# First pointwise weights kept in DRAM as two parts, three GpSimd convolution tiles and a layer norm spread over the last products

## The reference, cut to what matters

```python
mixed = concatenate([gla_o, hgrn_o, xo]) * silu(gate)       # 2048 wide
x = x + mixed @ w_out                                       # end of the first block; x = rms_norm(x)
mod = silu(c) @ w_mod + b_mod                               # six vectors of 1024
h = modulate(rms_norm_2(x, norm1_g), sh1, s1)
u = h @ w_pw1 + b_pw1                                       # 1024 -> 2048
a, gate = split(u); u = a * sigmoid(gate)
u = dwconv(u, w_dw) + b_dw                                  # 31 taps, in segments of 64 tokens
u = silu(layer_norm(u, ln_g, ln_b))
x = x + g1 * (u @ w_pw2 + b_pw2)
x = x + g2 * (square(relu(modulate(rms_norm_2(x), sh2, s2) @ w1)) @ w2)
```

## Time and profile before

| | before |
|---|---|
| median of 3 runs | 2215.16 us |
| profiled execution | 2215.97 us, its span 2214.2 us |
| PE busy | 2074.0 us (94%), 10286 matmuls |
| DVE busy | 1173.6 us (53%) |
| POOL busy | 867.5 us (39%) |
| ACT busy | 675.7 us (31%) |
| DMA | 171.59 MB, 77 GB/s over the span |

### The profile page before, as it was taken

One profiled execution on the slowest core, in us unless ns is written; L12 is line 12 of the kernel. 1 busy time (PEld: TensorE's weight loads), 2 busy tenths in 40 slices (PEclk: granted clock), 3 DMA queues, 4 the chain that ended last, 5 costly groups with the idle time before them and its releaser, 6 DMA issues.

```text
span 2214.2 us, 26275 instructions
## 1 busy us (share of the span) xinstructions
PE 2074.0 (94%) x10286; PEld 1728.3 (78%) x10286; DVE 1173.6 (53%) x1977; ACT 675.7 (31%) x1200; POOL 867.5 (39%) x511
## 2 busy tenths in 40 slices
PE   7899999898998889999989987899899999999997
PEld 5779988787887768888867866678778888888886
DVE  5353455456463346775578877989634222222226
ACT  2312322211036510010345436464433322212212
POOL 7352122211111343453439873679344442222120
PEclk9999999999999999999989997899999999999999
DMA  4111011101010354554122321222223231111112
GB/s 162 58 58 44 25 58 48 48 33 36 29 35 34 133 186 147 163 176 147 48 67 87 95 71 44 66 75 91 74 84 98 95 95 57 60 54 48 48 48 77
DMA packets 57323, 171.59 MB, mean 77 GB/s; under 512 B 6368, under 2 KB 6752, under 8 KB 57072
## 3 DMA queue, kind: packets, MB, share of 16 engines
q1 hardware_dynamic: 57200, 169.91, 23.6%
HBM read 157.30 MB, written 12.58 MB: 77 GB/s over the span
## 4 chain that ended last, share of the span: by engine, by line
PE 79%; DVE 10%; issue 4%; ACT 3%; POOL 2%; DMA 1%; SPq 0%; POOLq 0%; DVEq 0%; ACTq 0%
PE B L1153 38%; PE B L1336 23%; PE B L1219 6%; PE B L1257 4%; DVE B L1824 2%; POOL WL L2340 1%; DVE OSB L1827 1%; DMA MODRAW<-wmod 1%; DVE HB L1824 1%; DVE ACC L1821 1%; PE B L1418 1%; PE B L1281 1%; PE B L1284 1%; PE B L1297 1%; DVE RES L1824 1%
## 5 line engine op out<-in xcount | busy, mean ns | idle before, releaser
L1153 PE MATMUL B<-HB,WH 128*128 128x512 f32 x2976 | 943.6, 405 | 33.5 <-ACT WH L1527 12.9
L2340 POOL TENSOR_TENSOR WL<-RAW,WH 128x1024 fp32r<-128x1024 f32 x217 | 529.4, 2443 | 517.4 <-ACT WH L1527 510.8
L1153 PEld LDWEIGHTS B<-HB,WH 128*128 128x128 f32 x2976 | 559.4, 192 | 157.9 <-issue 33.2
L1153 PE MATMUL B<-HB,WL 128*128 128x512 f32 x1488 | 569.5, 397 | 10.1 <-POOL WL L2340 10.1
L1153 PEld LDWEIGHTS B<-HB,WL 128*128 128x128 f32 x1488 | 285.0, 192 | 75.1 <-POOL WL L2340 13.6
L1824 DVE SCALAR_TENSOR_TENSOR B<-UP,vec,B 128x512 f32<-128x512 f32 x336 | 226.5, 747 | 0.0
L1824 DVE SCALAR_TENSOR_TENSOR RES<-B,modv,RES 128x512 f32<-128x512 f32 x144 | 105.0, 747 | 201.6 <-PE B L1336 168.5
L2338 POOL TENSOR_SCALAR WH<-RAW 128x1024 fp32r<-128x1024 f32 x73 | 85.6, 1173 | 287.3 <-DMA RAW<-wall 287.3
L1527 ACT ACTIVATE WH<-RAW 128x1024 fp32r<-128x1024 f32 x144 | 150.5, 1051 | 152.2 <-DMA RAW<-wall 152.2
L2317 POOL TENSOR_TENSOR small<-small 128x4 f32<-128x4 f32 (+2 forms) x36 | 36.7, 1019 | 396.5 <-DVE small L1827 396.4
L1336 PE MATMUL B<-HIDH,WH 128*128 128x512 f32 x512 | 187.0, 398 | 0.0
(11 more groups left out here) (235 smaller groups left out, 2718.4 us busy)
## 6 DMA issues: line engine op xcount, KB each, us to landing
RAW<-wall SPq DMA_DIRECT2D x217, 512.0 KB, 3.5
MODRAW<-wmod SPq DMA_DIRECT2D x96, 256.0 KB, 2.8
RES<-xT SPq DMA_DIRECT2D x16, 512.0 KB, 7.1
oscr<-OT SPq DMA_DIRECT2D x32, 256.0 KB, 2.0
OI<-oscr SPq DMA_DIRECT2D x16, 512.0 KB, 3.3
outT<-RES SPq DMA_DIRECT2D x16, 256.0 KB, 2.1
mraw<-memT SPq DMA_DIRECT2D x1, 1024.0 KB, 13.2
mst<-masks SPq DMA_DIRECT2D x1, 224.0 KB, 14.1
```

The costliest lines, as they stand in the source:

```text
L1153: i = pe.matmul(bank, a[:, ks], hb(part, k, h), start=k == 0 and n == 0, stop=k == 7 and n == 2)
L2340: po.tensor_tensor(lo, raw, hi.bitcast(F32), ALU.subtract).then_inc(sig[f"w_lo{q % NW}"], 1)
```

## The change

Four parts.

1. **Ahead units.** Sixteen new units `("ahead", "pa"/"pg", f)` stand in the gates' stage, one behind each of the 16 units of groups 0 and 1. Each is loaded and split (both parts by GpSimd), and `put_back` (SP) writes `WH` and `WL` to a DRAM tensor `parts`. Where the 32 `pa`/`pg` units are used, they are no longer split: SP loads `hi` and `lo` from `parts` straight into `WH` and `WL`. A slot that held an ahead unit is free when both of its writes have landed (`d_back`).
2. **Three tiles for GpSimd** in half 0: 1, 3, 5; two (1, 5) in half 1 as before.
3. **Layer norm of half 0 beside the last products.** `conv_norm(0)` goes to the background at rate 1.4 in place of `means(0)`; `own_norm(0)` runs after tile 4. In `normed` the `ysum` matmuls lag six steps, and eight steps pass between `ln_r` and `ln_row`, for both halves. Buffers move so that half 1's results and temporaries don't need the end of the products: `COB` lies in the tile's own `UP` buffer, and waits change with them.
4. **The planner's figures**: a matmul 0.2275 us from the convolution on, a tap 0.67.

```diff
-BY_POOL = (1, 5)
+BY_POOL = ((1, 3, 5), (1, 5))
-COST = {"dve": {"glu": 0.75, "tap": 0.69, ...
+COST = {"dve": {"glu": 0.75, "tap": 0.67, ...
...
+    ahead = [("ahead", kind, f) for f in range(8) for kind in ("pa", "pg")]
     for g in range(NG):
-        plan += [("wo", g, j) for j in range(4)]
-        plan += [("gate", e) for e in range(4 * g + 5, min(4 * g + 9, 16))]
+        for u in [("wo", g, j) for j in range(4)] + [("gate", e) for e in range(4 * g + 5, min(4 * g + 9, 16))]:
+            plan.append(u)
+            if g < NG - 1 and ahead:
+                plan.append(ahead.pop(0))
...
+def is_split(unit):
+    return unit[0] in ("pa", "pg")
...
-        piece("split", q, hi_by[0])
+        if not is_split(UNITS[q]):
+            piece("split", q, hi_by[0])
...
     def u_get(*kind):
+        while is_ahead(UNITS[at_unit[0]]):
+            j = at_unit[0]
+            at_unit[0] += 1
+            u_advance(j)
+            piece("put_back", j)
+            ended[j] = ("put_back",)
...
+    pace[0] = 0.2275
...
     def normed(h):
         take(S, "ysum", h)
         for f in range(8):
             piece("ysub", f, h)
             piece("ysq", f, h)
-            if f:
-                piece("ysum", f - 1, h)
+            if f >= 6:
+                piece("ysum", f - 6, h)
             yield
-        if h == 0:
-            take(B, "r1_row", 0)
-            piece("r1_row", 0)
-            for f in range(8):
-                piece("pre", f, 0)
-        piece("ysum", 7, h)
-        yield
+        for f in range(2, 8):
+            piece("ysum", f, h)
+            yield
         piece("ln_r", h)
-        yield
-        yield
+        for _ in range(8):
+            yield
         take(S, "ln_row", h)
         piece("ln_row", h)
-        yield
...
-                piece("r1_dg", 0)
+            if f == 4 and not h:
+                drain()
+                bg.append(own_norm(0))
         if not h:
-            drain()
-            bg.append(means(0))
+            bg.append(conv_norm(0))
+            rate[0] = 1.4
...
     while bg:
+        now["pe"] = max(now["pe"], now["dve"])
         step_in(bg)
-    beside(normed(0), {9: 2, 10: 1})
...
         def wait_unit_read(w, q):
             name = ended[q]
-            if name[0] == "mv_end" and name[1] < 3:
+            if is_ahead(UNITS[q]):
+                w.wait_ge(sig[f"d_back{q % NW}"], 32 * back_n[q])
+            elif name[0] == "mv_end" and name[1] < 3:
...
-                    w.wait_ge(sig["tap"], n - 2)
+                    w.wait_ge(sig["tap"], n - 1 if h and k == TAPS - 1 else n - 2)
                     out_ = acc
                     if k == TAPS - 1:
                         out_ = seg(CO[h][f][:, :])
-                        if h:
-                            wait_product(w, 1)
-                        else:
+                        if h == 0:
...
             def load(q):
                 if q >= NW:
                     wait_unit_read(w, q - NW)
-                sp.dma_start(RAW[:, slot(q)], wall[WALL.index(contents(UNITS[q])), :, :]).then_inc(sig[f"d_raw{q % NW}"], 16)
+                if is_split(UNITS[q]):
+                    of = contents(UNITS[q])
+                    back = back_of[of]
+                    w.wait_ge(sig[f"d_back{back % NW}"], 32 * back_n[back])
+                    n = AHEAD_UNITS.index(of)
+                    sp.dma_start(WH[:, slot(q)].bitcast(F32), parts[n, 0, :, :]).then_inc(sig[f"d_hi{q % NW}"], 16)
+                    sp.dma_start(WL[:, slot(q)].bitcast(F32), parts[n, 1, :, :]).then_inc(sig[f"d_lo{q % NW}"], 16)
+                else:
+                    sp.dma_start(RAW[:, slot(q)], wall[WALL.index(contents(UNITS[q])), :, :]).then_inc(sig[f"d_raw{q % NW}"], 16)
+
+            def put_back(q):
+                n = AHEAD_UNITS.index(contents(UNITS[q]))
+                w.wait_ge(sig[f"w_hi{q % NW}"], raw_n[q])
+                sp.dma_start(parts[n, 0, :, :], WH[:, slot(q)].bitcast(F32)).then_inc(sig[f"d_back{q % NW}"], 16)
+                w.wait_ge(sig[f"w_lo{q % NW}"], raw_n[q])
+                sp.dma_start(parts[n, 1, :, :], WL[:, slot(q)].bitcast(F32)).then_inc(sig[f"d_back{q % NW}"], 16)
```

More of the change, by code:

```diff
@@ L34 @@
 WAIT = [4, 11, 3]
-BY_POOL = (1, 5)
+BY_POOL = ((1, 3, 5), (1, 5))
 AHEAD_GROUPS = 4
-COST = {"dve": {"glu": 0.75, "tap": 0.69, "taps_end": 0.7, "ysub": 0.7, "ln_r": 0.8, "z_mul": 0.7, "z_lo": 0.7, "pre": 0.75,
+COST = {"dve": {"glu": 0.75, "tap": 0.67, "taps_end": 0.7, "ysub": 0.7, "ln_r": 0.8, "z_mul": 0.7, "z_lo": 0.7, "pre": 0.75,
                 "pw2": 0.75, "sq_add": 0.7, "m1_mul": 0.75, "m1_lo": 0.75, "m2_mul": 0.75, "m2_lo": 0.75, "hid": 1.4,
@@ L98, in contents, with is_ahead @@
 def contents(unit):
-    return unit[:-1] if unit[0] in BY_TOKENS else unit
+    return unit[1:] if unit[0] == "ahead" else unit[:-1] if unit[0] in BY_TOKENS else unit
+def is_ahead(unit):
+    return unit[0] == "ahead"
+def is_split(unit):
+    return unit[0] in ("pa", "pg")
+AHEAD_UNITS = [u[1:] for u in UNITS if is_ahead(u)]
 WALL = list(dict.fromkeys(contents(u) for u in UNITS))
@@ L152, in make_plan @@
     lanes = {"dve": [], "pool": []}
-    hi_by, ahead = ["act"], [AHEAD]
+    hi_by, ahead, pace = ["act"], [AHEAD], [PASS]
     def u_split():
@@ L674, in means @@
                 piece("mean", f, h, len(left))
-                now["pe"] += 4 * PASS
+                now["pe"] += 4 * pace[0]
             yield
@@ L813, in first_hidden @@
             hidden(i, h)
+    rate[0] = 1.0
     second_product(0)
@@ L888, in wait_ge, with build_program @@
             self.seen[id(sem)] = count
-def build_program(nc, wall, wmod, xT, memT, vecs, gup, ident_d, masks_d, out, oscr):
+def build_program(nc, wall, wmod, xT, memT, vecs, gup, ident_d, masks_d, out, oscr, parts):
     es = ExitStack()
@@ L1034, in build_program @@
         CO = [[at(f"CO{f}", 512, F32, x0 + (2 + f) * K2) for f in range(8)],
[L1035 to L1037 removed]
+              [at(f"COB{f}", 512, F32, x0 + 18 * K2 + (8 + f) % 10 * UPW * 4 if f not in BY_POOL[1] else
+                  x0 + 21 * K2 + 10 * UPW * 4 if f == BY_POOL[1][0] else hb0 + (8 + f) * K4 + K2) for f in range(8)]]
+        YT = [[at(f"YT{h}{i}", 512, F32, (x0 + (10 + i) * K2, hb0 + (4 + i) * K4 + K2)[h]) for i in range(4)] for h in range(2)]
+        LNDG = [at(f"LNDG{h}", 512, F32, (x0 + 14 * K2, hb0 + 3 * K4 + K2)[h]) for h in range(2)]
         RL = at("RL", 512, F32, x0 + 16 * K2)
@@ L1070, in slot @@
             return slice(q % NW * 1024, q % NW * 1024 + 1024)
+        raw_n, parts_n, at_slot = {}, {}, Counter()
+        for q, u in enumerate(UNITS):
+            kind = "parts" if is_split(u) else "raw"
+            at_slot[kind, q % NW] += 1
+            (parts_n if is_split(u) else raw_n)[q] = at_slot[kind, q % NW]
+        back_n = {q: 1 + sum(is_ahead(UNITS[p]) for p in range(q % NW, q, NW)) for q, u in enumerate(UNITS) if is_ahead(u)}
+        back_of = {u[1:]: q for q, u in enumerate(UNITS) if is_ahead(u)}
         def generation(j):
@@ L1745, in ptap0 @@
                 up_ready(w, f, h)
-                if h:
+                if h and f != BY_POOL[1][0]:
                     wait_product(w, 1)
@@ L1765, in ysq @@
                 if h:
-                    wait_conv_over(w)
+                    wait_product(w, 1)
                 else:
@@ L2571 @@
     oscr = nc.dram_tensor("oscr", (16, 128, T), F32, kind="Internal").ap()
-    build_program(nc, *aps, out, oscr)
+    parts = nc.dram_tensor("parts", (len(AHEAD_UNITS), 2, 128, 1024), F32, kind="Internal").ap()
+    build_program(nc, *aps, out, oscr, parts)
     r = run_bass_kernel_spmd(nc, [arrays], core_ids=[0])
```

69 lines of the change are left out of this document (32 added, 37 removed).

## The result

The changed kernel takes 2271.7 us, the median of four runs (2259.1 to 2272.7), beside 2218.4 us for the kernel before on the same chip (2213.6 to 2224.4). The ratio is 1.0226, with a 95% interval of 1.018 to 1.0272. The forecast was 2228, the range 2186 to 2252: the direction was right, the size was not, and the time lies outside the range.

A forecast was written before the change was run, and what follows sets the result against it. PE was taken to bound the gates' stage (busy 295.9 of 296 us), with a hole in half 0's layer norm. On 2216.0 us, + 43 (ahead units) - 34.5 (convolution) + 3 (half 1) = + 12 gave 2228 us, range 2186 to 2252.

The forecast's parts named there:

- The ahead units' waits: Gates' stage, groups 0 and 1: PE waits for late real units cost 43 us, between 24.5 and 57.
- the stores: Gates' stage: two 512 KB stores per ahead unit, priced at 2 us each, delay SP's next loads; 18.5 us put on them.
- the real unit's load: Gates' stage: from SP's load of a real unit to GpSimd's start on it takes 3.8 us.
- The undisturbed bound: Gates' stage: lower bound of the ahead units' cost with SP not disturbed by stores, 24.5 us.
- pauses of some 3 us cost no clock: Gates' stage: after a 3.53 us pause PE's matmuls ran at once at their rate, after 7.38 not; no cost added.
- The exclusion of GpSimd and VectorE: Gates' stage: each fourth `mod` meeting a split waits it out, 2.83 against 0.75 us; cost 57 us, rival at 0.10.
- The rival of the hidden ahead units: Gates' stage: real units' loads go out early enough, only the convolution's gain is left, 2185 us; chance 0.14.
- the gain of 34.5 us: Convolution stage until `pw2` of half 0: 32 us from the earlier start, 2.5 from avoiding a long pause; bounds 24 and 43.5.
- The waits at the mean: Convolution stage, half 0: PE waits 9 us at the last mean, as it did before (8.3).
- Half 1: From `pw2` of half 0 on: mean planned too early loses 10 us, or a vanished pause gains 5; 3 lost taken.
- the first term: Sum of the forecast: the ahead units' cost in groups 0 and 1, + 43 us.

The follow-up runs named there:

- e8_no_stores: The changed kernel storing one ahead unit alone, the other fifteen loaded and split but not stored (first pointwise products left wrong): 2265.0 us, ratio 1.0193.
- e3_load_first: The changed kernel with SP issuing the load of the real unit behind an ahead unit before the four `mod` loads, not behind them: 2244.9 us, ratio 1.0134.
- e7_pace: The changed kernel with the planner's old figures (matmul 0.2133, tap 0.69) from `pw2` of half 0 on: 2246.3 us, ratio 1.0111.
- e5_real_first: e4_back_first with GpSimd's split of an ahead unit put behind that of the next real unit: 2227.6 us, ratio 1.0035.
- e4_back_first: e3_load_first with the ahead unit's two stores also issued ahead of the four `mod` loads: 2229.8 us, ratio 1.0071.

## Why the prediction was wrong, step by step

Against the profiled execution the forecast was + 11.5 us and the change brought + 56.5. Of the 45 us between them 10.2 lie in groups 0 and 1, 22.5 in the convolution stage, 7 in half 1, and 5.3 in stages that I had at nothing.

- **The ahead units' waits** were forecast at 43 us; they are 33.0. The chain was right: SP's load 10 us behind the unit's end (forecast 9.1 and 11.5), `WH` and `WL` from GpSimd, `RAW` from DMA. Single sizes were off both ways: the stores carry 9 us, not 18.5, and the real unit's load takes about 6 us to GpSimd's start in the turn shown, not 3.8. The undisturbed bound of 24.5 us of waits is near the 27.9 of e8_no_stores.
- **The step that failed in this stage is "pauses of some 3 us cost no clock".** It rested on one row, 3.53 us. Here PE pauses for `WH` and, within three microseconds, for `WL`, in seven turns, and the matmuls behind take double in all seven. That is 20.5 us, a term that the sum had at nothing; with it the stage costs 53.2 instead of 43. That this is only 10 off is partly luck, since the waits came out 10 too high. The trace of the kernel before had the warning, two pauses (and one of 0.58 us ahead of them) just before the convolution stage, with the lower clock behind them:

```profile
1118.26 0.77 PE L1153 MATMUL B<-HB,WH 128*128 128x512 f32 x1 [1.78 <-ACT HB L1713]
1120.53 0.80 PE L1153 MATMUL B<-HB,WH 128*128 128x512 f32 x1 [1.51 <-DVE HB L1824]
...
1121.55 1.05 PE L1153 MATMUL B<-HB,WH 128*128 128x512 f32 x2
```

And a lone pause of some 3 us is not safe either: in e3_load_first, ahead of the gates' stage, the lower clock follows on a lone pause that is shorter than 3.53 us:

```profile
788.33 1.22 PE L1193 MATMUL B<-HB,WH 128*128 128x512 f32 x2 [2.82 <-DVE GA L1858]
```

- **The exclusion of GpSimd and VectorE** is there: the `mod` pieces in groups 0 and 1 have a median of 1.34 us and reach 2.86, where one alone takes 0.75. It was a rival at 0.10 with a total cost of 57; taking the ahead units' splits off GpSimd brought the median back to 0.75 and gave back 16 us of waits and clock together. The Trainium skill's rule ("SBUF — State Buffer", section "SBUF: two separate sides") agrees with these rows; how large a part of the loss it is stays open.
- **The rival of the hidden ahead units** was to decide at a load 5 us behind the unit's end. e3_load_first put it there, and the groups still took 28 us more than before: stores in front of the slot, and the order of the splits, come next in line.
- **Convolution stage, the largest error.** The step that failed is the gain of 34.5 us. The products were to end 191 us after the first `glu`, and the last one starts at 192.0 (1390.94 less 1198.9). The waits at the mean are 4.1 us (1.15 and 2.97) and 3.5 for a row of the first norm, against 9. Yet the gain is 12.0 and not 34.5. Of the difference 10.5 is a misreading: I took 1365.6 as the start of `pw2`, from the last `z` in the chain, but its products had been running beside `z` since 1355.12; the 28 busy us of the window up to 1366 were in part these products, and not 12 us of `ysum` and else pause. Another 7.7 is the wait for `WH` on ScalarE, and PE comes out of it at the lower clock, where I had counted on 2.5 us for the upper; the 1.8 that are left lie in the products ahead of the wait. The order of ScalarE was not looked at.
- **Half 1** was forecast at 3 us lost, with 10 as the bound; it lost 10.0. The mechanism was the one named (by its new figures the planner puts the mean too early), and e7_pace bears it out: with the old figures 20 us come back. That is twice the loss, so the new order itself gains some 10 us there, which the sum did not have. The second wait, for VectorE's `HIDL`, was not foreseen.

In all: 43 became 53.2, -34.5 became -12.0, 3 became 10.0. The right direction rests on the first term, and there on two errors that half cancel.

## What to carry to other kernels

A queue of four slots that serves a second kind of work loses look-ahead for the first: count at which place of each queue the next needed load, and then the next needed split, comes to stand. Price a stall with what follows it, and from more than one row: here 33 us of short pauses took another 20 in slower matmuls. When work is moved beside products, look for what is queued behind it on the engine that does it; and read the end of a hole from the first matmul behind it, not from the last piece of the work that feeds it.

## What the runs showed of the hardware

- The length of a pause does not tell by itself whether the lower clock follows. Lone pauses of 3.53 us (before) and 2.50 (after, at 796.33) cost nothing, lone ones of 2.82 (e3_load_first), 1.17 (e5_real_first) and 7.38 (before) brought pairs of 1.05 to 1.22 us instead of 0.62. Of double pauses for `WH` and `WL` all seven of the changed kernel did it, also one of 1.34 and 1.11 us, while in e4_back_first two of three did not, among them 1.04 and 2.25 us. The granted clock of groups 0 and 1 was 0.90 with seven such turns and 0.98 before.
- Stores of 512 KB beside loads landed in 5.3 us in the median in the changed kernel (`parts<-WH`; 6.6 in e5_real_first), and 0.79 of the DMA engines' time and 267 GB/s (e5_real_first) left PE with 6.8 us of waits in 192: traffic as such was not what cost.
- A sigmoid and a `silu` that take turns on ScalarE cost 1.28 us for each turn (`ACT_TABLE_LOAD` at 1385.12 and 1388.07 in the changed kernel).
